# Two modulation groups moved from block 1's attention to the opening of block 2's scan

## The reference, cut to what matters

```python
def adaln_modulation(cond, w_ada, b_ada):
    return jnp.split(jax.nn.silu(cond) @ w_ada + b_ada, N_MOD, axis=-1)
...
        mods_lat = [m[:, None, :] for m in adaln_modulation(c, ada_w[layer], ada_b[layer])]
        mods_ctx = adaln_modulation(c_ctx, ada_w[layer], ada_b[layer])
        x = ffn_sublayer(x, *mods_lat[0:3], ffn_w_gu[layer, 0], ffn_w_down[layer, 0], ln_g[layer, 0], ln_b[layer, 0])
```

## Time and profile before

| | |
|---|---|
| Three runs | 3064.95, 3065.37, 3073.93 us, median 3065.37 |
| The profiled execution | 3073.82 us, span of its instructions 3071.8 |
| TensorE, matmuls | busy 2922.9 us, 95% of the span |
| DVE, ACT, POOL | busy 1562.2, 1079.9 and 22.8 us |
| Read from HBM | 475.49 MB, 155 GB/s over the span |
| Modulation matmuls, L2043 | 70.5 us busy in 576 instructions |

### The profile page before, as it was taken

One profiled execution on the slowest core, in us unless ns is written; L12 is line 12 of the kernel. 1 busy time (PEld: TensorE's weight loads), 2 busy tenths in 40 slices (PEclk: granted clock), 3 DMA queues, 4 the chain that ended last, 5 costly groups with the idle time before them and its releaser, 6 DMA issues.

```text
span 3071.8 us, 42579 instructions
## 1 busy us (share of the span) xinstructions
PE 2922.9 (95%) x17536; PEld 2304.4 (75%) x17536; DVE 1562.2 (51%) x2471; ACT 1079.9 (35%) x1705; POOL 22.8 (1%) x57
## 2 busy tenths in 40 slices
PE   8989999998999989999999998999989999998998
PEld 6668877766887768888544885788868888666898
DVE  4445478543545873243498655633345333315654
ACT  1433367343335752222303543322223222212433
POOL 0000000000000000000000000000000000000000
PEclk9999999999999999999999999999999999999999
DMA  6657789456667962222211104322222222120452
GB/s 219 242 208 280 269 316 355 182 221 226 256 261 309 353 229 97 103 92 105 96 56 69 71 3 159 103 104 92 100 83 85 96 96 96 55 83 29 164 178 96
DMA packets 69109, 478.89 MB, mean 156 GB/s; under 512 B 7376, under 2 KB 10832, under 8 KB 11728
## 3 DMA queue, kind: packets, MB, share of 16 engines
q1 hardware_dynamic: 67616, 473.16, 41.7%
q10 hardware_dynamic: 1328, 3.41, 0.3%
HBM read 475.49 MB, written 1.05 MB: 155 GB/s over the span
## 4 chain that ended last, share of the span: by engine, by line
PE 81%; PEld 5%; DVE 4%; ACT 4%; DMA 2%; issue 2%; PEldq 1%; DVEq 0%; ACTq 0%; SPq 0%
PE ps L649 19%; PE ps L650 19%; PE ps L651 19%; PE ps L641 9%; PEld ps L641 4%; PE ps L2372 2%; PE ps L2363 2%; PE ps L2043 2%; PE ps L1752 1%; PE ps L1767 1%; PE ps L982 1%; PE ps L2130 1%; DMA ring<-in_ada 1%; PE ps L1824 1%; DVE w_lo L679 1%
## 5 line engine op out<-in xcount | busy, mean ns | idle before, releaser
L679 DVE TENSOR_TENSOR w_lo<-ring,w_hi 128x1024 fp32r<-128x1024 f32 x560 | 680.4, 1223 | 694.0 <-ACT w_hi L662 688.5
L662 ACT ACTIVATE w_hi<-ring 128x1024 fp32r<-128x1024 f32 x558 | 589.3, 1060 | 854.6 <-PE ps L651 762.8
L649 PE MATMUL ps<-x_hi,w_hi 128*128 128x512 f32 (+1 forms) x1472 | 540.5, 367 | 28.9 <-DVE x_lo L1111 13.5
L650 PE MATMUL ps<-x_lo,w_hi 128*128 128x512 f32 (+1 forms) x1472 | 538.6, 366 | 0.0
L651 PE MATMUL ps<-x_hi,w_lo 128*128 128x512 f32 (+1 forms) x1472 | 538.5, 366 | 0.0
L649 PEld LDWEIGHTS ps<-x_hi,w_hi 128*128 128x128 f32 x1472 | 280.8, 191 | 76.9 <-issue 29.8
L650 PEld LDWEIGHTS ps<-x_lo,w_hi 128*128 128x128 f32 x1472 | 280.9, 191 | 43.8
L651 PEld LDWEIGHTS ps<-x_hi,w_lo 128*128 128x128 f32 x1472 | 280.4, 190 | 44.2
L641 PE MATMUL ps<-HM,ring 128*128 128x256 f32 (+1 forms) x864 | 267.0, 472 | 8.6 <-ACT HM L1100 6.3
L649 PE MATMUL ps<-h_hi,w_hi 128*128 128x512 f32 (+1 forms) x704 | 255.2, 362 | 0.0
L650 PE MATMUL ps<-h_lo,w_hi 128*128 128x512 f32 (+1 forms) x704 | 255.2, 362 | 0.0
(11 more groups left out here) (419 smaller groups left out, 3985.7 us busy)
## 6 DMA issues: line engine op xcount, KB each, us to landing
ring<-in_moe_up SPq DMA_DIRECT2D x128, 1024.0 KB, 5.4
ring<-in_ff_up SPq DMA_DIRECT2D x88, 1024.0 KB, 4.7
ring<-in_ada SPq DMA_DIRECT2D x72, 1024.0 KB, 4.9
ring<-in_moe_down SPq DMA_DIRECT2D x64, 1024.0 KB, 5.6
ring<-in_ff_down SPq DMA_DIRECT2D x44, 1024.0 KB, 4.7
ring<-in_w_in SPq DMA_DIRECT2D x14, 1024.0 KB, 6.0
ring<-in_even_in SPq DMA_DIRECT2D x10, 1024.0 KB, 4.8
ring<-in_w_o SPq DMA_DIRECT2D x8, 1024.0 KB, 7.8
```

The source lines that it names most:

```text
L649: pe.matmul(dst, hi, xh, start=start, stop=False, skip_group_check=True)
L650: pe.matmul(dst, hi, xl, start=False, stop=False, skip_group_check=True)
L662: act.activation(w_hi[:, j % HALVES, :], ring[:, u % SLOTS, (j % 2) * D:(j % 2 + 1) * D], ACT.Copy)\
L679: dve.tensor_tensor(w_lo[:, j % HALVES, :], ring[:, u % SLOTS, (j % 2) * D:(j % 2 + 1) * D], w_hi[:, j % HALVES, :].bitcast(F32), ALU.subt ...
```

## The change

The site `attend_first` is taken out of block 1, in both layers, and the site `scan` takes three groups instead of one. The code of the attention stays as it is; it asks whether it has such a site (`first`) and issues nothing where there is none. In the scan's opening TensorE now does product, turn, product, turn, product; the third turn stands behind the first level's Y, and the wait for the kept values behind that. ACT does the rows and the kept copies of the three groups one after the other. There are 18 groups still; since the groups are numbered by their place, each site behind the first one taken out works on a group of weights with a lower number than now, up to the scan's.

```diff
--- before.py
+++ after.py
@@ -544,7 +544,6 @@
             stage(n + "rope", pe=["swapped"])
             modulation_site(n + "rope", 4, (2, 3))
             stage(n + "attend", pe=PE_UNITS, act=ACT_UNITS, dve=DVE_UNITS)
-            modulation_site(n + "attend_first", 4, (6, 7))
             modulation_site(n + "attend_last", 4, (2, 3))
             out_stage(n + "out", w["w_o"][l])
             ln_stage(n + "ln1", True)
@@ -577,7 +576,7 @@
                 stage(n + "rows", pe=["k0", "v0", "k1", "v1", "sums", "k2", "v2", "k3", "v3"],
                       act=["k0", "v0", "k1", "v1", "k2", "v2", "sums", "k3", "v3"], dve=["sums"])
                 stage(n + "scan", **scan_marks())
-                modulation_site(n + "scan", 4, (1, 5), n + "rows")
+                modulation_site(n + "scan", 3 * MOD_GROUP, (1, 5), n + "rows")
                 stage(n + "merge", pe=["turned"], act=["sq", "inverse"], dve=["sums", "ready"])
                 modulation_site(n + "merge", 4, (4, 5))
             else:
@@ -2422,7 +2421,9 @@
             for d in range(2):
                 pe.wait_ge(dve_done, st.v("dve", f"mt0.{d}"))
                 turned(0, d)
-            modulation_turn(pe, site_banks[n], g)
+            for e in range(2):
+                modulation_turn(pe, site_banks[n], g + e)
+                modulation_product(pe, site_banks[n], g + e + 1)
             for i in range(4):
                 last = i == 3
                 for j in range(1, LEVELS):
@@ -2464,7 +2465,8 @@
                             pe.wait_ge(dve_done, st.v("dve", f"R3.{d}"))
                             from_state(3, d)
                     if j == 1 and i == 0:
-                        pe.wait_ge(mod_kept, g + 1)
+                        modulation_turn(pe, site_banks[n], g + 2)
+                        modulation_kept(pe, n)
                     for d in range(2):
                         b, m = 4 * d, DN[d]
                         pe.wait_ge(act_done, st.v("act", f"Y{i}.{j}.{d}"))
@@ -2524,8 +2526,9 @@
             for d in range(2):
                 act.wait_ge(pe_done, st.v("pe", f"GC0.{d}"))
                 spread_gate(1, d)
-            modulation_rows(act, copy, site_banks[n], g)
-            modulation_keep(act, copy, site_banks[n], g)
+            for e in range(3):
+                modulation_rows(act, copy, site_banks[n], g + e)
+                modulation_keep(act, copy, site_banks[n], g + e)
             for i in range(4):
                 last = i == 3
                 for j in range(1, LEVELS):
```

## The result

The changed kernel takes 3077.92 us (median of its runs, 3076.27 to 3081.1) against 3066.23 for the kernel before in the same series: a ratio of 1.0030, with a 95% interval of 1.0017 to 1.0043, that is 5 to 13 us more. In a second series, beside other runs of before, it was 3078.62 against 3067.93, 1.0031 (1.0021 to 1.0040). Forecast were 3080, the range 3070 to 3090, and slower. Lines of the changed program are lower by one (the product is L2042, the transposes of the attention L1173, the scan's levels L2371). Its profiled execution took 3077.92 with a span of 3076.0.

A forecast was written before the change was run, and what follows sets the result against it. The prediction took TensorE as the bound, its matmul side busy for 95% of the span. Scan costs 20.2 + 1.3 + 3.4 = 24.9 less 10.2 in the attention gave +14.7 on 3065.37: 3080 us, range 3070 to 3090.

The forecast's parts named there:

- The attention: Head of block 1's attention: unit 1's transposes start 4.9 us sooner in layer 0, 5.4 or 0.2 less in layer 1; 10.2 taken.
- its 0.6: Attention, layer 0: VectorE's row maxima start 4.28 us sooner, 0.6 less than TensorE gains; VectorE makes this up in later units.
- The loads: Scan's opening: TensorE waits for the second and third groups' loads, ending about 9.4 and 19.3 us behind level 1's old start; 20.2 us.
- a slow spell of the transfers: Start of the opening's loads: a slow spell of about 1 us may come twice or not at all, plus or minus 1.
- in time: Rival, scan's opening: loads arrive in time, only the work of 10.5 us counts, less 10.2: 3066, no change; chance 0.12.
- The turn between level 1's steps: Scan's opening: third group's transposes and copies lengthen level 1's start to second step from 1.19 to about 2.5 us: 1.3.
- The clock: Scan's opening: granted clock at 0.50 when the third group ends, costing 3.4 us, bounded by 0 and about 6.5.
- The first rival: Scan's opening: the clock stays at 2.4 GHz since each wait is short; 3077 us, chance 0.18.
- The rate: Scan's opening: third group's loads follow at the queue's rate, some 420 GB/s, 2.5 us each.
- The sum: Whole kernel: 24.9 us more in the scan less 10.2 in the attention, +14.7, giving 3080.
- the terms may be added to any median: Whole kernel: the terms don't depend on which execution is taken, so +14.7 is added to the median, 3065.37.

The follow-up runs named there:

- the filler: Changed kernel plus one unit-matrix matmul by 512 columns ahead of each unit's product in the opening's second and third group: 3076.90 us, 1.0031 to the kernel before.
- Without the loads: Changed kernel with the opening's second and third group multiplied from the first group's weights, eight 1 MB loads less: 3063.90 us, 0.9986 to the kernel before.
- the one-group kernel: Kernel before with only layer 1's group moved into the scan's opening, layer 0's staying in its attention: 3077.30 us, 1.0028 to the kernel before.

## Why the prediction was right

**The attention.** Forecast 10.2, found 10.06 (4.76 + 5.30). What was left is TensorE's own row of work, and DVE made up its 0.6: set side by side, the two traces keep layer 0's gain to the end of the attention.

**The loads.** In before's order level 1 starts 5.23 us behind the first product's start, here that is 1693.07. The two loads were forecast to end 9.4 and 19.3 behind it and ended 8.1 and 19.3 behind it. The second time was met with luck: the second group's loads came 1.3 us sooner than forecast, and the third group's took 11.2 instead of 10, since the last of them was late:

```profile
1708.71 1.06 PE L2042 MATMUL ps<-ring,tmp 128*32 128x512 f32 x8 [0.43 <-DMA ring<-in_ada]
1712.43 1.94 PE L2042 MATMUL ps<-ring,tmp 128*32 128x512 f32 x8 [2.66 <-DMA ring<-in_ada]
```

It isn't a slow spell of the transfers, such as the forecast allowed for: the rate beside it is 424 GB/s. A load counts as landed when sixteen completion events are in; of this one's the trace has fifteen by 1711.10 and the sixteenth at 1712.39. The 10.88 that the forecast took from the attention ends on such a load too (fifteen by 110.51, the sixteenth at 111.55). Level 1 starts at 1714.37, 21.3 behind; without the 0.9 that the last quarter lost to the clock (1.94 against 1.06 with the filler), 20.4, and forecast were 20.2. Without the loads the opening costs 9.7: the rival "in time" had the right price (10.5) for a case that isn't this one.

**The turn between level 1's steps.** Forecast 1.3; 3.66 instead of 1.19 is 2.47, of which 0.82 (1.90 against 1.08) and 0.48 (1.06 against 0.58) are the clock's. That leaves 1.2.

**The clock.** Forecast 3.4; the last quarter 0.9, level 1's first step 0.82, the turn 0.48 and the second step 1.57 make 3.8, and in the opening the filler gave back 3.5. The first rival is out by this, and not by the time: its 3077 is nearer to 3077.92 than the forecast's 3080. The Trainium skill ("TensorE: Matmul & The Clock Gate", section "HAM oscillation — how this bites in real kernels") describes matmuls shorter than the DMA waits between them and a clock that falls; the trace agrees, with 0.50 in two stretches of the opening, behind quarters of 1.06 with waits of up to 1.43 and then of 2.66. By the Trainium skill's rule there on single long gaps, on which the first rival stood, the clock would have stayed up; the trace doesn't bear that out here.

**The rate.** The rate of the earlier trace rows held: 424 GB/s in the waits. The Trainium skill's bound of about 358 GB/s for transfers from HBM ("DMA: Bandwidth & Descriptors", section "Where 436 GB/s comes from") is passed by this trace.

**The sum.** The two places cost 25.3 less 10.06, +15.2, against a forecast of +14.7. The medians differ by 11.7 and 10.7, with intervals that end at 13.2 and 12.3. So 3.5 to 4.5 us were gained elsewhere, and here the forecast's claim that the terms may be added to any median was too simple.

The same gain is in all seven comparisons of a kernel without layer 0's group in its attention: opening less attention comes to 2.1 to 5.2 us more than the medians differ by (for the kernel that only leaves the groups out, -10.1 against -13.7). In the three kernels that keep that group it is 0.1 to 2.3. It has the size of a clock that is up longer. Before's 27 executions of the second series have a mean granted clock of 0.9826, and run from 3062 us at 0.985 to 3076 at 0.980, some 2.6 us for each 0.001. The changed kernel's nine have 0.9812, although 17 us at 0.50 in the opening take off 0.0028 by themselves. So, if all nine have the opening of the two profiles, the clock was 0.0014 higher elsewhere: an estimated 3.6 us.

In the two profiles the clock is at 0.50 for 120.7 us before (one of its longer executions) and 110.8 after, 17.1 of these in the opening. One place of the difference is layer 0's router: the earlier trace rows has 6.54 for its product, the changed kernel this (TensorE's timeline):

```profile
189.81 3.64 PE L2042 MATMUL ps<-ring,tmp 128*32 128x512 f32 x32
```

In the profiles of the four kernels that keep layer 0's group in the attention, before among them, this product took 5.00 to 6.54; in the seven profiles without it 3.64 four times, and 5.01 to 6.52 three times. Why the change lets the clock be up there more often was tested by no run; it stays open.

## What to carry to other kernels

A piece of work with its own loads costs where it stands, not by its instructions: such a group cost 5 us in the attention, 10 to 15 in an opening that has to wait for its loads, and nothing in a gap whose loads were issued before. Before moving work, look for where its buffers come free and count the transfers behind that point at the queue's rate. And where the clock falls in a gap, work moved there can give back more than it cost in its old place: here 2.4 us on top of 5.3.

## What the runs showed of the hardware

- No wait in the opening was longer than 2.82 us, and yet the granted clock fell to 0.50: in the one-group kernel behind waits of 1.33 and 2.82 us between quarters of 1.06, so that the next quarter took 1.93. With 0.95 us of filler ahead of each quarter it read 1.00 throughout.
- The filler's f32 matmul of 128x128 by 128x512 took 0.95 us in two instructions, 0.48 each; the 32 instructions of a group's product, with 32 columns of weights each and four side by side, take 3.57 together, 0.11 each.
- In each of these streams one load is late without a dip in the rate: the wait of 2.82 above, where those beside it are 0.55 and 1.33, and the 2.66 of the changed kernel. Fifteen of its sixteen completion events come in time and the last one some 1.3 us later (1708.41 and 1709.79 in the one-group kernel). Ahead of it the trace has a packet of 16 KB on the queue that the views name `q8 instruction` (from 1707.28, 0.93 us; in the changed kernel from 1708.20, 1.06 us). The order is the same in the traces of the kernel with one filler and of the changed kernel's second run; that the one causes the other was not tested.
